# Second pass of a hybrid encoder layer: PSUM banks and copies of the transposed inverse's products

## What is computed

```python
def step(state, inp):                       # per head, state 64 x 64
    r_t, w_t, k_t, v_t, a_t, b_t = inp
    sa = jnp.einsum('bhvk,bhk->bhv', state, a_t)
    state = (state * w_t[:, :, None, :] + sa[..., None] * b_t[:, :, None, :]
             + v_t[..., None] * k_t[:, :, None, :])
    y = jnp.einsum('bhvk,bhk->bhv', state, r_t)
    return state, y
```

## Time and profile before

| | us |
|---|---|
| Three runs | 2858.02, 2862.46, 2865.93 |
| Median | 2862.46 |
| The profiled execution | 2862.2 |
| Its span, first to last instruction | 2860.2 |
| TensorE matmuls busy | 2483.3 |
| Products of L1107 in pass 2 | 298.1 |
| ScalarE busy | 733.6 |
| VectorE busy | 1079.2 |

### The profile page before, as it was taken

How to read it: one execution, slowest core, us unless ns; L and a number is a source line. 1 busy time by engine, 2 the same in 40 slices (tenths; PEclk the granted TensorE clock), 3 DMA queues, 4 the chain that set the end, 5 groups by cost and what they waited for, 6 DMA issues and landing times. The chain is left out here.

```text
span 2860.2 us, 68640 instructions
## 1 busy us (share of the span) xinstructions
PE 2483.3 (87%) x28334; PEld 1604.6 (56%) x28335; DVE 1079.2 (38%) x2622; ACT 733.6 (26%) x1782; POOL 406.3 (14%) x455
## 2 busy tenths in 40 slices
PE   3999999999997699999999995589999999989800
PEld 1888888888886567777777773323333333323200
DVE  0344544545445245656565554211111111111118
ACT  0244343443443113222222221012222222212200
POOL 0212112121121011212121210000000000000013
PEclk7999999999997899999999996599999999999955
DMA  8011121121123823232323210745535679999597
GB/s 318 8 68 66 45 88 47 45 89 45 45 82 121 335 80 108 103 123 83 126 91 113 91 69 37 320 180 220 220 132 220 268 270 362 349 426 358 204 369 284
DMA packets 59767, 472.50 MB, mean 165 GB/s; under 512 B 8284, under 2 KB 9344, under 8 KB 38944
## 3 DMA queue, kind: packets, MB, share of 16 engines
q1 hardware_dynamic: 39432, 403.49, 36.3%
q0 software_dynamic: 9936, 36.18, 3.6%
q10 hardware_dynamic: 10184, 29.67, 2.7%
HBM read 373.90 MB, written 95.42 MB: 164 GB/s over the span
## 5 line engine op out<-in xcount | busy, mean ns | idle before, releaser
L1726 PE MATMUL ps<-arena 128*32 128x512 f32 x4608 | 516.4, 605 | 35.2 <-DMA arena<-wex 35.2
L452 PE MATMUL ps<-arena 128*128 128x128 f32 (+2 forms) x3584 | 419.7, 276 | 2.1 <-ACT arena L601 2.1
L452 PEld LDWEIGHTS ps<-arena 128*128 128x128 f32 (+2 forms) x3584 | 406.9, 186 | 17.0 <-ACT arena L601 13.0
L1726 PEld LDWEIGHTS ps<-arena 128*32 128x32 f32 x4608 | 151.3, 112 | 393.6 <-issue 366.7
L1107 PE MATMUL ps<-arena 64*64 64x64 f32 x8704 | 298.1, 222 | 30.4 <-ACT arena L1310 9.1
L1107 PEld LDWEIGHTS ps<-arena 64*64 64x64 f32 x8704 | 278.0, 136 | 59.1 <-issue 58.0
L1740 PE MATMUL ps<-arena 128*32 128x512 f32 x2304 | 263.8, 598 | 18.1 <-DMA arena<-wex 16.8
L1252 PE MATMUL ps<-arena 128*128 128x512 f32 x512 | 238.9, 610 | 0.7 <-ACT arena L1329 0.7
L1946 DVE TENSOR_TENSOR arena<-arena,ps 128x256 f32<-128x256 f32 x72 | 29.9, 415 | 456.3 <-ACT arena L1785 456.3
L1785 ACT ACT_TABLE_LOAD x36 | 46.2, 1283 | 603.8 <-PE ps L1726 603.8
L463 PE MATMUL ps<-arena 128*128 128x256 f32 (+1 forms) x512 | 174.3, 488 | 0.0
(11 more groups left out here) (321 smaller groups left out, 3033.3 us busy)
## 6 DMA issues: line engine op xcount, KB each, us to landing
arena<-wex SPq DMA_DIRECT2D x108, 2048.0 KB, 9.6
mid<-arena SPq DMA_DIRECT2D x16, 2568.0 KB, 8.5
arena<-mid SPq DMA_DIRECT2D x16, 2568.0 KB, 10.4
arena<-ada SPq DMA_DIRECT2D x12, 2048.0 KB, 11.6
y<-arena ACTq DMA_DIRECT2D x36, 512.0 KB, 8.0
arena<-x SPq DMA_DIRECT2D x31, 512.0 KB, 5.4
arena<-w_in SPq DMA_DIRECT2D x8, 1232.0 KB, 25.6
y<-arena SPq DMA_DIRECT2D x16, 512.0 KB, 11.3
```

Source lines behind the costliest of these rows:

```text
L452: mm = pe.matmul(bank[name][0:m, at:at + P], V["w_in"][:, kk, w0:w0 + m], V["hT"][:, kk, :], start=(kk == 0), stop=(kk == KD - 1))
L1726: mm = pe.matmul(bank[("HA", "HB")[g]][rows[j], :], xT[:, kk, rows[j]], slot[j][:, at:at + 2 * FH], start=(kk == 0), stop=(kk == KD - 1))
```

## The change

The transposed products (Z times XT) of levels 1 to 5 go to columns 0 to 255 of banks YE and YO instead of columns 256 to 511 of X0 and X1. Each block marks its own bank full. ScalarE copies X and XT by instructions of their own, 256 columns each, in the order X0, X1, YE, YO. TensorE issues the same products in the same order; its waits are: for XT of the level before, the read of YE or YO; for the banks, X and then YE or YO, each ahead of its own block. `Wt` waits for the last read of YE and YO.

```diff
-         "X0": ("M", "t0", *(f"x{l}" for l in _LV), "WT"),
-         "X1": ("M", "t0", *(f"x{l}" for l in _LV), "WT", "D0", "D1"),
-         "YE": ("y",), "YO": ("y",),
+         "X0": ("M", "t0", *(f"x{l}" for l in _LV[:-1]), "WT"),
+         "X1": ("M", "t0", *(f"x{l}" for l in _LV[:-1]), "WT", "D0", "D1"),
+         "YE": (*(f"xT{l}" for l in _LV), "y"), "YO": (*(f"xT{l}" for l in _LV), "y"),
...
+    XT_BANKS = ("YE", "YO")
...
-            def blocks(name, lhs, rhs, heads, at=0, first=True, last=True):
-
-                if first:
-                    pe.sem_inc(S["pe_passed"], 1)
+            def blocks(name, lhs, rhs, heads):
+
+                pe.sem_inc(S["pe_passed"], 1)
                 for i, h in enumerate(heads):
                     for rows in chunk:
-                        mm = pe.matmul(bank[name][rows, at + CHUNK * i:at + CHUNK * i + CHUNK], lhs(rows, h), rhs(rows, h),
+                        mm = pe.matmul(bank[name][rows, CHUNK * i:CHUNK * i + CHUNK], lhs(rows, h), rhs(rows, h),
                                        start=True, stop=True)
-                if last:
-                    B.full(mm, name)
+                B.full(mm, name)
...
                         B.wait_read(pe, f"Z{g}", f"z{l}", n)
-                        B.wait_free(pe, f"X{g}", f"x{l}", n)
+                        if l == 1:
+                            B.wait_read(pe, f"X{g}", "t0", n)
+                        else:
+                            B.wait_read(pe, XT_BANKS[g], f"xT{l - 1}", n)
                         if l < last:
-                            blocks(f"X{g}", XT, lambda rows, h: Z[rows, h, :], heads, last=False)
-                        blocks(f"X{g}", lambda rows, h: Z[rows, h, :], XT, heads, at=256, first=(l == last))
+                            B.wait_free(pe, f"X{g}", f"x{l}", n)
+                            blocks(f"X{g}", XT, lambda rows, h: Z[rows, h, :], heads)
+                        B.wait_free(pe, XT_BANKS[g], f"xT{l}", n)
+                        blocks(XT_BANKS[g], lambda rows, h: Z[rows, h, :], XT, heads)
...
-                    B.wait_read(pe, f"X{g}", f"x{last}", n)
+                    B.wait_read(pe, XT_BANKS[g], f"xT{last}", n)
...
             def Xl(l):
-                o = 1 if l == last else 0
-
                 def go(n, b):
-                    for g in range(2):
-                        B.wait_full(act, f"X{g}", f"x{l}", n)
-                        B.free(act.activation(XX[:, g, o:, :], split(bank[f"X{g}"][:, 256 * o:], 2 - o), ACT.Copy), f"X{g}")
+                    for o, names, use in ((0, ("X0", "X1"), f"x{l}"), (1, XT_BANKS, f"xT{l}")):
+                        for g, name in enumerate(names if o or l < last else ()):
+                            B.wait_full(act, name, use, n)
+                            B.free(act.activation(XX[:, g, o, :], bank[name][:, 0:256], ACT.Copy), name)
```

## The result

The changed kernel takes 2888.36 us (median; 2887.41 to 2890.30), the kernel before beside it 2863.15 (2858.02 to 2865.93): a ratio of 1.0091, 95% interval 1.0074 to 1.0108. The forecast was 2857.8 in a range of 2850 to 2865. It is slower by 25 us where 5 us less were expected.

What follows compares the result with a forecast made beforehand. The second pass was taken as bound by TensorE. From 2862.2 us, 4.65 us of removed waits, with added work counted as nothing, left 2857.55; adjusted toward the runs' median, the forecast was 2857.8, range 2850 to 2865.

Steps and rivals of the forecast that it cites:

- Pace: TensorE's stream of small products without a border: 0.029 us an instruction, 0.47 us a block of 16.
- Removed: TensorE's wait for ScalarE's copy before Z goes; VectorE's eviction limits the gain to 0.15 us at 31 places, 4.65 us.
- Added on ScalarE: Four 256-wide copies replace two 512-wide in levels 1 to 4: 21 us more work over 15 tiles, hidden by idle time.
- the banks YE and YO: Added waits for these banks: 7 us to spare at level 1, 0.12 us before Yv, so no cost.
- Added: semaphore work on TensorE's queue: 26 more waits and passes a tile on TensorE, bounded by nothing and 0.11 us each; taken as nothing.
- D: Rival: TensorE's queue is near its limit, each added semaphore step delays products; 2879.3 us at 0.055 us each; chance 0.05.
- B: Rival: the whole 0.40 us stop of the loads goes at 31 places, 12.4 us, giving 2850.1 us; chance 0.07.

Runs made afterwards that it cites:

- e3: Changed kernel without the waits that others imply and without the second block's pe_passed, banks and copies kept: 2857.3 us, 0.9986 of the kernel before.
- e4: Kernel before plus 256 semaphore increments among the output projection's wide products: 2858.5 us, 0.9993 of the kernel before.
- e5: Changed kernel with the added waits kept only where TensorE goes from Z to X, none between the X and XT blocks: 2854.3 us, 0.9981 of the kernel before.
- e12: e3 plus one increment in front of each wait for Z at the Z-to-X borders, 160 in all: 2859.7 us, 0.9996 of the kernel before.
- e13: e3 plus the pe_passed increment between the X and XT blocks of level 4 alone, 32 in all: 2860.3 us, 0.9981 of the kernel before.
- e15: e3 plus two increments between the X and XT blocks of levels 1 to 4, 256 in all: 2893.1 us, 1.0077 of the kernel before.
- e14: e3 plus the pe_passed increment between the X and XT blocks of levels 2 and 3, 64 in all: 2874.2 us, 1.0036 of the kernel before.

## Why the prediction was wrong, point by point

- *Pace.* Right: 0.030 us a load across three borders, as before.
- *Removed.* Right. The 31 waits and 9.1 us are gone, the stop before X is 0.25 us (forecast 0.26), a tile without a long stop is 0.35 us shorter (forecast 0.3), and e3 gives 4.0 us (1.1 to 7.2) where 4.65 were forecast. The waits for VectorE's eviction didn't rise by 31 in the matmuls' row (19 after 23): most of these stops stand in the row of the loads, as "issue".
- *Added on ScalarE; the banks YE and YO.* Right that it costs nothing, but too large: 21 us more work were forecast, 10.5 came, since copies that follow one another overlap (three of 386 ns in 0.94 us). No product waits for ScalarE in the waits of after, and `Yv` has no idle time ahead of it after, either:

```profile
L1179 PE MATMUL ps<-arena 64*64 64x64 f32 x448 | 15.9, 218 | 0.0
```

- *Added: semaphore work on TensorE's queue.* This is the step that failed. I gave bounds of nothing and 0.11 us each and took nothing, since a run of 96 matmuls crosses three borders at full pace. The pace between stops was the wrong thing to read: it is the same in the kernel after. The cost doesn't come at each instruction but in a few stops of up to 2.1 us, one fetched block apart, and in a lower clock behind them. It measures (2888.4 - 2857.3)/288 = 0.108 us each, the upper bound. The count was off as well, 26 steps a tile where 18 instructions came of it (a wait and the increment behind it share one), but that is small beside the price.
- *The rivals.* It was D, "the queue is so near its limit that each added semaphore step delays the products", to which I gave 0.05. Its price per step at which the kernel turns slower, 0.034 us, was exceeded threefold, though not by each step: e4, e5, e12 and e13 add 32 to 256 of them at no clear cost. B stayed away for the reason given, VectorE's eviction of Z comes next; the Trainium skill (Perfetto Trace Analysis, "Matmuls"), cited there, speaks of VectorE's evacuation as well as of ScalarE's. There was a row for it in before: nine stops of "issue" of the same products, 3.6 us, inside a stream in which nothing should be waited for. I had read only the rows of that view that name an engine.
- *The range.* It ended at 2865, below D, though the high bound of one unknown cost alone reached far above it: 390 x 0.11 = 43 us, 2901 (with the 288 that came of it 32 us, 2889). The range should take in the bounds of unknown costs; this one had been left out on the strength of the pace.

## What to carry to other kernels

In a stream of small products, count the semaphore instructions that stand by themselves on the engine's queue, and let waits ride on the products; here that gave 0.9%, where the two banks alone gave 0.35 us a tile, and 288 added ones lost 31 us. Before adding a step to such a queue, look in the profile for stops of "issue" in the middle of a run: here they stood where the supply of instructions was near its limit. And when a cost has only bounds, the pace of an undisturbed run excludes a cost per instruction, but no rare long stop.

## What the runs showed of the hardware that I had not expected

- TensorE can run out of instructions in straight code: stops of up to 2.8 us (e15), at the borders of blocks of 256 instructions, 16 KB, in streams where a load and its matmul take 0.030 us.
- The same semaphore instruction costs 0.22 us in one place (e14) and nothing measurable in three others (e4, e5, e13).
- In two stops of after the next block's transfer began 3.6 and 3.4 us after TensorE had resumed, with the DMA engines idle or 95% busy, and TensorE went on 2.6 and 2.4 us after it.
- A stop of 2.08 us was followed by a run at 0.044 us a matmul (4.18/96) instead of 0.032, at a granted clock of 0.97 over its 50 us.
